# Low parts of four weight blocks and the transpose of the global group's keys, moved to GpSimd and VectorE

## The chip, the cores and the metric

The kernel runs on one core of one Trainium2 chip. A core has a matrix engine (TensorE, PE in the profile, with its weight loads as PEld), a vector engine (VectorE, DVE), an activation engine (ScalarE, ACT), a general engine (GpSimd, POOL) and a queue engine that here issues all DMAs (SyncE, SP). Each runs its own instructions in the order in which they were written, and they wait for each other through semaphores. The metric is the device time of one execution in microseconds (us); lower is better.

## The reference

A trunk of two layers over 256 tokens of width 1024, all in float32. Each layer:

- `h = rms_norm(x)`, then one projection to 2304 columns, which gives q, k, v of two groups of heads. Group A (MoBA, called the global group here) has 8 heads of 64 with their own keys; since the block size is 256 and the sequence 256, it is plain causal attention. Group B (SWA) has 8 query heads on 2 key/value heads, a window of 128 and one learned sink per head.
- rotary positions on q and k of both groups, softmax attention in each, an `rms_norm` of each group's output, and the output projection of the two side by side, normed and added to x.
- a SwiGLU block: gate and up projections to 2816 columns, `silu(gate) * up`, the down projection, normed and added to x.

## The kernel before

**Split products.** Every float32 product on PE is made of three: operands are split into a high part (rounded to the PE's fp32r type) and a low part (what is left), and high x high, high x low and low x high are accumulated. The weights come from memory in 46 blocks per layer (`BLOCKS`), each 128 x 2048: blocks 0 to 8 are the input projection, 9 to 12 the output projection, then gate/up and down. A block b is loaded by SP into one of three places of `raw` (`load_block`, L345 to L349), ACT copies it to the high part `w_h` (`hi`, L530 to L543), DVE subtracts to the low part `w_l` (`lo`, L790 to L794), and PE multiplies with both (`multiply`, L1147). `w_h` and `w_l` have four places each; `slot` gives the place, `before` the block that held it last. SP may load a block when the low part of the block three before it is made (`lo_ready`), ACT may copy it when PE has used the block four before.

**The order of work** is written out by hand for each engine. The projections come out in five pieces ci = 0 to 4 (SWA keys and values, SWA queries, MoBA keys, MoBA queries, MoBA values) for two tiles t of 128 tokens. Blocks 5 and 6 hold the MoBA queries (ci 3), 7 and 8 the MoBA values (ci 4). For each piece DVE runs `project` (L839: gain and bias, L855) and `rotate` (L860: the rotary products L877 and L878 and their sums L881 and L883, all four with both operands in SBUF), and counts `rotated`. PE then transposes the result with four 128 x 128 transposes (`qk`, L1225, through `transpose`, L1217), and ACT copies them from PSUM to `qT` or `kT` (`keep_qk`, L596 to L603). Bank 6 of PSUM holds all these in turn (`HOLDS`, L152).

**Attention** runs in three rounds per group (`ROUNDS`: tile 0, then two halves of tile 1). In each, PE makes `scores` (L1229), DVE the masked maxima (`maxima`, L902), ACT the exponentials into `probs` (`exps`, L614), PE transposes them (`probs_transposed`), ACT copies (`keep_probsT`, L630), and PE multiplies with the values (`values`, L1269). `normalise` (DVE, L920 to L922) divides by the sums: for SWA it first adds the sink's part to the row sums (L920, both operands in SBUF). ACT sums the squares (`sum_o`, L640), POOL makes the reciprocal root (`rms_o`, L485 to L491), DVE scales (`scale_o`, L932), PE transposes (`mix`).

**POOL** otherwise does only the roots of the norms in this stage. In the feed-forward stage it carries 32 x 128 pieces between partition groups (`exchange`, L493 to L503): there DVE transposes within 32 x 32 squares (`squares_f`, L983) and POOL's 16 copies per piece (L501) put the squares where a full transpose has them.

**The orders around the change.** On DVE in layer 0: `maxima(SWA, 0)`, `project(1, 1)`, the low parts of blocks 5 and 6, `normalise(SWA, 0)`, `maxima(SWA, 1)`, `project(2, 0)`, `project(2, 1)`, `project(3, 0)`, `maxima(SWA, 2)`, the low part of 7, `scale_o(SWA, 0)`, the low part of 8, `project(3, 1)`. In layer 1 `project(2, 0)` and the low part of 6 stand before `normalise(SWA, 0)`. On PE: `qk(1, 1)` follows `probs_transposed(SWA, 0, 1)`, then half of a block, `values(SWA, 0, ...)`, `scores(SWA, 1)`, and later `probs_transposed(SWA, 1, ...)`. On ACT the high part of block 7 follows `keep_qk(1, 1)`; the high part of 8 follows `exps(SWA, 1)` in layer 0 and the high part of 7 in layer 1.

Of the kernel before, what the change touches and what calls it, by code (L numbers as in the profile page):

```python
# [65 lines left out]

RAW = 3
# [78 lines left out]
for j in range(2):  # L146
    HOLDS[4 + j].append(("ht", 0, j, 1))
    for g in (SWA, MOBA):
        for r in range(3):
            HOLDS[4 + j] += [("scores", g, r, j), ("pt", g, r, j)]  # L150
    HOLDS[4 + j].append(("ht", 1, j, 1))
HOLDS[6] += [("ht", 0, 0, 0), ("qk", 0, 0), ("qk", 1, 0), ("qk", 0, 1), ("qk", 1, 1), ("qk", 2, 0), ("qk", 2, 1),  # L152
             ("qk", 3, 0), ("qk", 3, 1), ("mix", SWA, 0), ("mix", SWA, 1), ("mix", MOBA, 0), ("mix", MOBA, 1),
# [5 lines left out]
def trunk(nc, x_in, b_in, g_attn_pre, g_attn_post, g_moba, g_swa, sinks_in,  # L159
# [3 lines left out]
    with ExitStack() as ctx:  # L163
# [33 lines left out]
        squares = [work[:, 2 + t, :] for t in range(T)]  # L197
        crossed = [work[:, 4 + t, :] for t in range(T)]
# [44 lines left out]
        lo_ready = sem("lo_ready")  # L243
        block_used = sem("block_used")
# [20 lines left out]
        squares_ready = [sem(f"squares_ready{t}") for t in range(T)]  # L265
        crossed_in = [sem(f"crossed_in{t}") for t in range(T)]
# [61 lines left out]

        def tokens(t):
            return slice(t * P, (t + 1) * P)  # L330
# [8 lines left out]
        def _(sp):  # L339
# [5 lines left out]
            def load_block(L, b, wait=True):  # L345
                r = slot(b, RAW)
                if wait:
                    place_free(lo_ready, L * NB + before(b, RAW) + 1)
                sp.dma_start(raw[:, r, :], w_blocks[L, b]).then_inc(raw_in[r], 16)  # L349
# [35 lines left out]
            for L in range(depth):  # L385
                for b in range(RAW + 1, NB):
                    load_block(L, b)
                    if b == 6:
# [3 lines left out]

                        sp.dma_start(gain_b[:], broadcast(g_attn_post[L], D)).then_inc(gain_b_in, 16)
# [6 lines left out]
                    if b == 11:  # L400
                        projected(L, 2, 1)
                        load_bias(L, 4)
                    if b == 15:
# [26 lines left out]
        def _(pool):  # L430
# [73 lines left out]

            pool.wait_ge(const_ready, 8)
            rms_x(0, 0, 0)
            rms_x(0, 0, 1)
            for L in range(depth):
                rms_o(L, SWA, 0)
                rms_o(L, SWA, 1)  # L510
# [19 lines left out]
        def _(act):  # L530
# [65 lines left out]
            def keep_qk(L, ci, t):  # L596
# [3 lines left out]
                dst = (kT[SWA], qT[SWA], kT[MOBA], qT[MOBA])[ci]  # L600
# [71 lines left out]
            for L in range(depth):  # L672
# [27 lines left out]
                keep_qk(L, 2, 0)  # L700
                exps(L, SWA, 2)
                sink_exps(L, 1)
                keep_qk(L, 2, 1)
# [76 lines left out]
        def _(dve):  # L780
# [9 lines left out]
            def lo(L, b):  # L790

                dve.wait_ge(hi_ready, L * NB + b + 1)
# [67 lines left out]
            def rotate(L, ci, t, n):  # L860
# [6 lines left out]
                if (ci, t) in ((2, 1), (3, 0), (3, 1)):  # L867
                    past = {(2, 1): (1, 0), (3, 0): (1, 1), (3, 1): (2, 0)}[ci, t]
                    held = BANK_OF[("qk", *past)]
                    dve.wait_ge(full[held], HELD[held].done(L, ("qk", *past)))  # L870
# [5 lines left out]
                                     for m in (stage, rope_tmp))  # L876
# [7 lines left out]
                                        ALU.add).then_inc(rotated, 1)  # L884

# [121 lines left out]
            for L in range(depth):  # L1007
                if L == 0:
# [11 lines left out]
                    project(L, 2, 0)  # L1020
                else:
# [10 lines left out]
                    project(L, 2, 0)  # L1032
                    after(L, 2)
                    normalise(L, SWA, 0)
                    maxima(L, SWA, 1)
                project(L, 2, 1)
                if L:
                    after(L, 3)
                project(L, 3, 0)
                maxima(L, SWA, 2)  # L1040
# [427 lines left out]
```

## Time and profile before

| | us |
|---|---|
| median of 3 runs | 576.99 (576.70 to 577.41) |
| the profiled execution | 576.57 |
| its span, first to last instruction | 574.8 |
| PE busy in it | 566.5 (99%) |
| DVE busy | 374.3 (65%) |
| ACT busy | 293.9 (51%) |
| POOL busy | 232.3 (40%) |
| mean granted TensorE clock | 0.998 of full speed |

The span leaves out 1.8 us around the instructions. Busy is the union of an engine's instructions; matmuls are pipelined, and their ends are modelled, so that the start-to-start distance of two matmuls is what one costs.

### The profile page before, as it was taken

The page shows a single profiled execution, that of the slowest core. Times are in us where ns is not written, and L with a number is a line of the kernel's source. Part 1 is how long each engine was busy: PE and PEld are TensorE (multiplying, and loading weights), DVE is VectorE, ACT ScalarE, POOL GpSimd, SP SyncE. Part 2 cuts the span into 40 slices and gives each one's busy share as a digit, 9 for nine tenths or more (in the row PEclk, how much of TensorE's full clock was granted, in tenths as well). Part 3 has the DMA queues.
Part 4 walks back from the last instruction along what each step waited for, and adds up shares of the span by engine and source line. Part 5 has one row for each costly group of instructions (what it writes and reads, how often), then busy time and mean ns, then how long its engine had stood idle before and what let it go on. Part 6 is the DMA issues. An engine that isn't in the chain of part 4 may idle for free.

```text
span 574.8 us, 8319 instructions
## 1 busy us (share of the span) xinstructions
PE 566.5 (99%) x3107; PEld 467.0 (81%) x3107; DVE 374.3 (65%) x486; ACT 293.9 (51%) x420; POOL 232.3 (40%) x452
## 2 busy tenths in 40 slices
PE   8999999999999999999999999999999999999996
PEld 6777877888888889888888888778888888898884
DVE  6789875946745747265597987576846746645722
ACT  7575755664345354163546655674644354325420
POOL 1100001607797797800120000043297797799100
PEclk9999999999999999999999999999999999999999
DMA  8953642538555550478265443516565564352701
GB/s 304 389 205 123 237 148 109 222 114 315 202 211 196 175 215 29 193 285 303 91 238 200 158 164 131 201 47 247 218 258 192 174 217 178 119 220 81 286 1 74
DMA packets 18729, 107.32 MB, mean 187 GB/s; under 512 B 2816, under 2 KB 3072, under 8 KB 7168
## 3 DMA queue, kind: packets, MB, share of 16 engines
q1 hardware_dynamic: 18688, 106.78, 50.3%
q8 instruction: 25, 0.41, 0.3%
q14 instruction: 16, 0.13, 0.1%
HBM read 105.72 MB, written 1.05 MB: 186 GB/s over the span
## 4 chain that ended last, share of the span: by engine, by line
PE 88%; DVE 6%; DMA 3%; ACT 1%; issue 1%; DVEq 0%; POOLq 0%; SPq 0%; POOL 0%; ACTq 0%
PE bank L1177 81%; PE bank L1217 4%; DMA raw<-in_w_blocks 3%; PE bank L1269 2%; PE bank L1242 2%; DVE w_l L793 1%; DVE bank L902 1%; DVE work L855 1%; DVE work L877 1%; DVE work L878 1%; DVE work L943 0%; DVE w_l L807 0%; ACT w_h L543 0%; DVE work L883 0%; ACT work L592 0%
## 5 line engine op out<-in xcount | busy, mean ns | idle before, releaser
L793 DVE TENSOR_TENSOR w_l<-raw,w_h 128x2048 fp32r<-128x2048 f32 x90 | 206.1, 2298 | 115.5 <-ACT w_h L543 115.4
L1177 PE MATMUL bank<-w_h,actT_h 128*128 128x512 f32 (+1 forms) x600 | 230.3, 384 | 0.4 <-DVE work L855 0.3
L543 ACT ACTIVATE w_h<-raw 128x2048 fp32r<-128x2048 f32 x90 | 171.9, 1915 | 110.0 <-PE bank L1177 90.1
L1177 PE MATMUL bank<-w_h,actT_l 128*128 128x512 f32 (+1 forms) x600 | 225.6, 376 | 0.0
L1177 PE MATMUL bank<-w_l,actT_h 128*128 128x512 f32 (+1 forms) x600 | 225.2, 375 | 0.0
L501 POOL COPY work<-work 32x128 f32<-32x128 f32 (+1 forms) x384 | 191.6, 499 | 75.4 <-DVE work L983 59.6
L1177 PEld LDWEIGHTS bank<-w_h,actT_h 128*128 128x128 f32 x600 | 113.1, 188 | 23.6 <-issue 2.2
L1177 PEld LDWEIGHTS bank<-w_h,actT_l 128*128 128x128 f32 x600 | 112.9, 188 | 21.0
L1177 PEld LDWEIGHTS bank<-w_l,actT_h 128*128 128x128 f32 x600 | 113.1, 189 | 18.8
L488 POOL TENSOR_TENSOR norms<-norms,constants 128x1 f32<-128x1 f32 x8 | 1.5, 193 | 146.8 <-ACT bank L640 146.8
L1177 PE MATMUL bank<-w_h,fT_h 128*128 128x512 f32 x160 | 49.4, 390 | 0.0
L1177 PE MATMUL bank<-w_h,fT_l 128*128 128x512 f32 x160 | 49.3, 389 | 0.0
L1177 PE MATMUL bank<-w_l,fT_h 128*128 128x512 f32 x160 | 49.3, 389 | 0.0
L614 ACT ACTIVATE work<-bank,neg_max 128x128 f32<-128x128 f32 (+1 forms) x64 | 26.0, 426 | 23.3 <-DVE neg_max L902 23.2
L1177 PEld LDWEIGHTS bank<-w_h,fT_l 128*128 128x128 f32 x160 | 30.0, 188 | 6.3
L1177 PEld LDWEIGHTS bank<-w_l,fT_h 128*128 128x128 f32 x160 | 30.0, 188 | 6.2
L1177 PEld LDWEIGHTS bank<-w_h,fT_h 128*128 128x128 f32 x160 | 29.8, 188 | 6.0
L478 POOL TENSOR_TENSOR norms<-norms,constants 128x1 f32<-128x1 f32 x8 | 6.7, 836 | 69.2 <-ACT work L592 69.2
L578 ACT ACTIVATE fT_h<-work 128x512 fp32r<-128x512 f32 x20 | 12.5, 624 | 40.6 <-POOL work L501 40.6
L1217 PE MATMUL bank<-ident,work 128*128 128x128 f32 x228 | 32.5, 274 | 0.7 <-ACT work L614 0.5
L1217 PEld LDWEIGHTS bank<-ident,work 128*128 128x128 f32 x228 | 26.6, 140 | 7.8 <-ACT work L614 1.7
L990 DVE TENSOR_TENSOR fT_l<-work,fT_h 128x512 fp32r<-128x512 f32 x20 | 14.5, 725 | 19.1 <-ACT fT_h L578 19.1
(77 smaller groups left out, 403.1 us busy)
## 6 DMA issues: line engine op xcount, KB each, us to landing
raw<-in_w_blocks SPq DMA_DIRECT2D x90, 1024.0 KB, 4.8
bias<-in_b_in SPq DMA_DIRECT2D x8, 256.0 KB, 5.6
raw<-in_w_blocks SPq DMA_DIRECT2D x4, 256.0 KB, 5.2
raw<-in_w_blocks SPq DMA_DIRECT2D x2, 512.0 KB, 7.6
x<-in_x SPq DMA_DIRECT2D x2, 512.0 KB, 10.5
gain_b<-in_g_attn_post SPq DMA_DIRECT2D x2, 512.0 KB, 7.4
bias<-in_g_ffn_pre SPq DMA_DIRECT2D x2, 512.0 KB, 5.5
gain_b<-in_g_ffn_post SPq DMA_DIRECT2D x2, 512.0 KB, 5.8
```

The costliest lines, as they stand in the source:

```text
L478: link(L, nc.gpsimd.tensor_tensor(ss_y[:, t, 0:1], ss_y[:, t, 0:1], eps, ALU.add))
L501: ins = nc.gpsimd.tensor_copy(crossed[t][32 * j:32 * j + 32, i * n:(i + 1) * n], squares[t][32 * i:32 * i + 32, j * n:(j + 1) * n])
L543: nc.scalar.activation(w["h"][:, slot(b), :], raw[:, r, :], ACT.Copy).then_inc(hi_ready, 1)
L578: nc.scalar.activation(f_part("h", c, t), f_view(c, t), ACT.Copy).then_inc(f_hi_ready, 1)
L614: last = nc.scalar.activation(probs[:, j, n * keys:(n + 1) * keys], bank[4 + j][:, n * keys:(n + 1) * keys], ACT.Exp, bias=neg_max[:, g, t ...
L793: nc.vector.tensor_tensor(w["l"][:, slot(b), :], raw[:, slot(b, RAW), :], w["h"][:, slot(b), :].bitcast(F32), ALU.subtract).then_inc(lo_re ...
L855: nc.vector.scalar_tensor_tensor(dst[:, 0:n], bank[b][:, 0:n], rstd_x[:, t:t + 1], bias[:, ci % 2, 0:n], ALU.mult, ALU.add).then_inc(drain ...
L990: nc.vector.tensor_tensor(f_part("l", c, t), f_view(c, t), f_part("h", c, t).bitcast(F32), ALU.subtract).then_inc(f_lo_ready, 1)
L1177: ins = nc.tensor.matmul(bank[BANK_OF[name]][:, 0:n], left[s][:, at + k, tokens(t)], right[r][:, k, c * BANK:c * BANK + n], start=first an ...
L1217: ins = nc.tensor.transpose(out_[:, q * P:(q + 1) * P], src(q), ident[:])
L1242: ins = nc.tensor.matmul(bank[4 + j][:, n * keys:(n + 1) * keys], qT[g][side, i, tokens(t)], kT[g][side, i if g == MOBA else 0, 0:keys], s ...
L1269: ins = nc.tensor.matmul(bank[b][rows, h * HEAD:(h + 1) * HEAD], probsT[:, j, at + side * HEAD:at + (side + 1) * HEAD], v[g][:, kb, cols], ...
```

## The change

Four things. POOL computes the low parts of blocks 5 to 8 of each layer, as the first instructions of its layer, and signals them on a semaphore of its own; DVE's `lo` skips them; PE and SP wait for whichever engine makes the block's low part. The MoBA keys (ci 2) are no longer transposed by PE and copied by ACT: DVE transposes their 32 x 32 squares into `gain_b`, and POOL carries the squares to `kT` with 16 copies per tile, the two tiles between `rms_o(SWA, 0)` and `rms_o(SWA, 1)`. The load of `gain_b` (the gain after attention) moves on SP's queue from behind block 6 to behind block 11, where it waits for both tiles' keys; block 12 and all that follow on the queue stand behind it. On DVE `maxima(SWA, 2)` moves ahead of `project(3, 0)`.

```diff
+POOL_LOW = (5, 6, 7, 8)
...
+        k_squares = [gain_b[:, t * GROUP:(t + 1) * GROUP] for t in range(T)]
...
+        def low_done(L, b):
+            mine = [c for c in range(NB) if (c in POOL_LOW) == (b in POOL_LOW)]
+            return pool_lo_ready if b in POOL_LOW else lo_ready, L * len(mine) + mine.index(b) + 1
...
@@ SP: load_block, and the load of gain_b
-                    place_free(lo_ready, L * NB + before(b, RAW) + 1)
+                    last = before(b, RAW)
+                    place_free(*low_done(L + last // NB, last % NB))
...
                     if b == 6:
...
-                        sp.dma_start(gain_b[:], broadcast(g_attn_post[L], D)).then_inc(gain_b_in, 16)
...
                     if b == 11:
                         projected(L, 2, 1)
                         load_bias(L, 4)
+                        place_free(k_crossed, T * (L + 1))
+                        sp.dma_start(gain_b[:], broadcast(g_attn_post[L], D)).then_inc(gain_b_in, 16)
...
@@ POOL
+            def lo(L, b):
+                pool.wait_ge(hi_ready, L * NB + b + 1)
+                nc.gpsimd.tensor_tensor(w["l"][:, slot(b), :], raw[:, slot(b, RAW), :],
+                                        w["h"][:, slot(b), :].bitcast(F32), ALU.subtract).then_inc(pool_lo_ready, 1)
+
+            def cross_k(L, t):
+                pool.wait_ge(k_squares_ready, T * L + t + 1)
+                pool.wait_ge(rstd_o_ready, R_O.done(L, (SWA, 0)))
+                square = k_squares[t].rearrange("p (i c b) -> p i c b", i=4, b=32)
+                for a in range(4):
+                    for c in range(4):
+                        at = t * P + 32 * a
+                        ins = nc.gpsimd.tensor_copy(kT[MOBA][32 * c:32 * c + 32, :, at:at + 32],
+                                                    square[32 * a:32 * a + 32, :, c, :])
+                ins.then_inc(k_crossed, 1)
+                pool.wait_ge(k_crossed, T * L + t + 1)
...
             for L in range(depth):
+                lo(L, 5)
+                lo(L, 6)
+                lo(L, 7)
+                lo(L, 8)
                 rms_o(L, SWA, 0)
+                cross_k(L, 0)
+                cross_k(L, 1)
                 rms_o(L, SWA, 1)
...
@@ ACT
-                keep_qk(L, 2, 0)
...
-                keep_qk(L, 2, 1)
...
@@ DVE
             def lo(L, b):
+                if b in POOL_LOW:
+                    return
...
+            def square_k(L, t):
+                dve.wait_ge(rotated, turned(L, (2, t)))
+                nc.vector.transpose(k_squares[t], roped[2, t]).then_inc(k_squares_ready, 1)
...
                     project(L, 2, 0)
+                    square_k(L, 0)
...
                 project(L, 2, 1)
+                maxima(L, SWA, 2)
+                square_k(L, 1)
                 if L:
                     after(L, 3)
                 project(L, 3, 0)
-                maxima(L, SWA, 2)
...
@@ PE
-                        pe.wait_ge(lo_ready, L * NB + b + 1)
+                        pe.wait_ge(*low_done(L, b))
...
-                for name in (last_q, last_k):
-                    landed(L, name)
+                landed(L, last_q)
+                if g == SWA:
+                    landed(L, last_k)
+                else:
+                    pe.wait_ge(k_crossed, T * L + t + 1)
...
-                qk(L, 2, 0)
...
-                qk(L, 2, 1)
```

## Rows read from the trace of the kernel before

**Rows 1.** The page, part 4: the chain that ended last, shares by engine.
```profile
PE 88%; DVE 6%; DMA 3%; ACT 1%; issue 1%; DVEq 0%; POOLq 0%; SPq 0%; POOL 0%; ACTq 0%
```

**Rows 2.** Who PE waited for: total us, times, longest; the second largest of three.
```profile
PE bank L1217 <- ACT work L614: 0.5, 2, 0.3
```

**Rows 3.** Timeline of PE around one group of four transposes: start, length, engine, line.
```profile
28.86 0.40 PE L1177 MATMUL bank<-w_l,actT_h 128*128 128x512 f32 x1
29.10 0.39 PE L1177 MATMUL bank<-w_h,actT_l 128*128 128x512 f32 x1
...
30.00 0.39 PE L1177 MATMUL bank<-w_l,actT_h 128*128 128x512 f32 x1
```

**Rows 4.** Low parts and square transposes on DVE; copies on POOL (ns min/median/max).
```profile
L793 DVE TENSOR_TENSOR w_l<-raw,w_h 128x2048 fp32r<-128x2048 f32 x90 | 206.1, 2298 | 115.5 <-ACT w_h L543 115.4
...
L983 DVE STREAM_TRANSPOSE work<-work 128x512 f32<-128x512 f32 x20 | 14.0, 702 | 0.0
...
L501 POOL COPY work<-work x384: 226/288/2442, 132.5 to 532.4; 32x128 f32<-32x128 f32 x160, 32x64 f32<-32x64 f32 x32
```

**Rows 5.** Timeline, narrow windows of the feed-forward stage: POOL copies beside DVE's low parts.
```profile
134.16 0.28 POOL L501 COPY work<-work 32x128 f32<-32x128 f32 x1
...
134.23 2.36 DVE L793 TENSOR_TENSOR w_l<-raw,w_h 128x2048 fp32r<-128x2048 f32 x1 [1.14 <-ACT w_h L543]
...
134.48 2.26 POOL L501 COPY work<-work 32x128 f32<-32x128 f32 x1
...
529.92 2.32 DVE L793 TENSOR_TENSOR w_l<-raw,w_h 128x2048 fp32r<-128x2048 f32 x1
530.13 2.20 POOL L501 COPY work<-work 32x64 f32<-32x64 f32 x1
```

**Rows 6.** Timeline of layer 0, 30 to 47 us, by engine (ACT, DVE, PE).
```profile
30.46 3.71 ACT L543 ACTIVATE w_h<-raw 128x2048 fp32r<-128x2048 f32 x2
...
39.16 1.91 ACT L543 ACTIVATE w_h<-raw 128x2048 fp32r<-128x2048 f32 x1
44.21 0.48 ACT L614 ACTIVATE work<-bank,neg_max 128x256 f32<-128x256 f32 x1 [3.13 <-DVE neg_max L902]
...
35.78 0.69 DVE L877 TENSOR_TENSOR work<-work,sin 128x512 f32<-128x512 f32 x1
...
37.45 0.42 DVE L883 TENSOR_TENSOR work<-work 128x256 f32<-128x256 f32 x1
...
42.19 0.16 DVE L920 TENSOR_TENSOR row_sum<-row_sum,sink_exp 128x8 f32<-128x8 f32 x1
...
37.55 1.04 PE L1217 MATMUL bank<-ident,work 128*128 128x128 f32 x8
...
39.90 1.15 PE L1269 MATMUL bank<-v_swa,work 128*64 128x64 f32 x32
...
46.27 0.49 PE L1217 MATMUL bank<-ident,work 128*128 128x128 f32 x3
```

**Rows 7.** Timeline of layer 1, 307 to 328 us, by engine (ACT, DVE, PE).
```profile
307.68 1.92 ACT L543 ACTIVATE w_h<-raw 128x2048 fp32r<-128x2048 f32 x1 [0.41 <-PE bank L1177]
...
320.49 3.71 ACT L543 ACTIVATE w_h<-raw 128x2048 fp32r<-128x2048 f32 x2
...
315.26 0.69 DVE L877 TENSOR_TENSOR work<-work,sin 128x512 f32<-128x512 f32 x1
...
322.49 0.16 DVE L920 TENSOR_TENSOR row_sum<-row_sum,sink_exp 128x8 f32<-128x8 f32 x1
...
318.89 1.04 PE L1217 MATMUL bank<-ident,work 128*128 128x128 f32 x8
...
327.60 0.38 PE L1217 MATMUL bank<-ident,work 128*128 128x128 f32 x2
```

**Rows 8.** Start-up matmuls of PE (busy us, mean ns); the last stretch (its PEclk is 0.78).
```profile
L1211 PE MATMUL bank<-work 128*128 128x512 bf16 x10 | 4.4, 631 | 1.5 <-DVE work L993 1.5
...
569.20:574.80 5.60, 0.00 (x0) 0.00 (x0) 2.12 (x4) 0.65 (x2) 0.74 (x2) 0.78 0.25 95
```

More of the change, by code:

```diff
@@ L151 @@
     HOLDS[4 + j].append(("ht", 1, j, 1))
-HOLDS[6] += [("ht", 0, 0, 0), ("qk", 0, 0), ("qk", 1, 0), ("qk", 0, 1), ("qk", 1, 1), ("qk", 2, 0), ("qk", 2, 1),
-             ("qk", 3, 0), ("qk", 3, 1), ("mix", SWA, 0), ("mix", SWA, 1), ("mix", MOBA, 0), ("mix", MOBA, 1),
+HOLDS[6] += [("ht", 0, 0, 0), ("qk", 0, 0), ("qk", 1, 0), ("qk", 0, 1), ("qk", 1, 1), ("qk", 3, 0), ("qk", 3, 1), ("mix", SWA, 0), ("mix", SWA, 1), ("mix", MOBA, 0), ("mix", MOBA, 1),
              ("ht", 1, 0, 0)]
@@ L243, in trunk @@
         lo_ready = sem("lo_ready")
+        pool_lo_ready = sem("pool_lo_ready")
         block_used = sem("block_used")
@@ L265, in trunk @@
         squares_ready = [sem(f"squares_ready{t}") for t in range(T)]
+        k_squares_ready = sem("k_squares_ready")
+        k_crossed = sem("k_crossed")
         crossed_in = [sem(f"crossed_in{t}") for t in range(T)]
@@ L599, in keep_qk @@
                 act.wait_ge(full[b], HELD[b].done(L, ("qk", ci, t)))
-                dst = (kT[SWA], qT[SWA], kT[MOBA], qT[MOBA])[ci]
+                dst = {0: kT[SWA], 1: qT[SWA], 3: qT[MOBA]}[ci]
                 n = dst.shape[1]
@@ L868, in rotate @@
                     past = {(2, 1): (1, 0), (3, 0): (1, 1), (3, 1): (2, 0)}[ci, t]
-                    held = BANK_OF[("qk", *past)]
-                    dve.wait_ge(full[held], HELD[held].done(L, ("qk", *past)))
+                    if past == (2, 0):
+                        dve.wait_ge(k_squares_ready, T * L + 1)
+                    else:
+                        held = BANK_OF[("qk", *past)]
+                        dve.wait_ge(full[held], HELD[held].done(L, ("qk", *past)))
                 dve.wait_ge(drained[b], HELD[b].done(L, ("proj", ci, t)) + 1)
@@ L1032, in _ @@
                     project(L, 2, 0)
+                    square_k(L, 0)
                     after(L, 2)
@@ L1233, in scores @@
                 last_q, last_k = (("qk", 1, t), ("qk", 0, t)) if g == SWA else (("qk", 3, t), ("qk", 2, t))
[L1234 to L1235 removed]
+                landed(L, last_q)
+                if g == SWA:
+                    landed(L, last_k)
+                else:
+                    pe.wait_ge(k_crossed, T * L + t + 1)
                 for j in range(2):
```

## The prediction, made before the changed kernel had run

> **What bounds the kernel now.** I read the chain that ended last first: 88% of it is PE [rows 1], and the table of times has PE busy for 566.5 of 574.8 us. The list of waits comes next, and for this stage it holds one entry, 0.5 us for ACT's exponentials [rows 2]. So PE is fed without a pause, and only two things can move the time: instructions that leave PE, and waits that arrive at it. DVE's 65% is no bound, and what it is freed of is worth nothing by itself. But PE runs in a written order, and some of DVE's results reach it with almost nothing to spare, so after the chain I read the timelines at those places [rows 6, 7].
>
> **What leaves PE.** Four groups of four transposes (MoBA keys, two tiles, two layers). Two neighbouring matmuls start 0.23 to 0.24 us apart; with four transposes between, the second matmul after them starts 0.90 us after the one ahead of them [rows 3]. 0.90 less two such distances (0.46) is 0.44 us for a group, and four groups are 1.76 us, all on the path. ACT loses four copies that nobody on the path waits for: nothing.
>
> **What moves from DVE to POOL.** DVE loses eight low parts of 2.3 us (18.4 us) and gains four square transposes of 0.70 us [rows 4]. Neither is on the path. POOL gains eight two-operand instructions of 128 x 2048 and 64 copies. A copy of 128 elements takes 288 ns (median), one of 64 takes 226 ns (the least) [rows 4]: 0.97 ns an element and 0.16 us fixed. A subtraction of 2048 elements is at least 2.15 us (if both operands stream together) and 4.1 us if they come one after the other. The trace has no large two-operand instruction on POOL. I take 4.1, since every row there is a one-operand copy at one element in 0.97 ns, and keep 2.15 as the lower end. The Trainium skill (GPSIMD Engine Reference, section 3.1) says the two read streams share one port and gives 4497 ns for this size; by it each would be 0.4 us longer, and the sum about 1 us higher.
>
> By plain durations all of it is hidden. In layer 0 block 5's high part ends at 32.4 and 6's at 34.2 [rows 6]; POOL would end their low parts at 36.5 and 40.7, and PE takes block 5 at 42.1 and block 6 behind it. The 16 copies of a tile start 0.33 us apart (134.16 and 134.48 [rows 5]), 5.3 us a tile.
>
> **The port.** Rows 5 say more. A POOL copy that starts at 134.48, while DVE subtracts (134.23 to 136.59), takes 2.26 us in place of 0.29: it stands still until DVE has ended. The other direction is there too: the copy ahead started at 134.16, and DVE's subtraction, which started 0.07 us later, took 2.36 against 2.29 us; it was held until about 0.14 us into the copy, half its length, which is its reading. Both engines want one read path when DVE reads two operands from SBUF, and whoever has it keeps it. And they alternate: at 529.92 DVE goes from one subtraction into the next, and the copy that had waited gets in between. DVE instructions with one operand in PSUM (L855, the maxima, L922) aren't touched.
>
> With copies this costs DVE 0.1 us. With POOL subtractions of 4.1 us it costs up to 4 us for one DVE instruction, and the four of `rotate`, `scale_o`, and L920 of `normalise` are of that kind. The Trainium skill (SBUF — State Buffer, section "Who interferes with whom") states it as a lock that the first one holds for its whole instruction, which speaks against this change; the trace agrees for copies (2.26 us for 0.29) and shows nothing of POOL holding it long.
>
> **Layer 0, worked out.** The low part of 5 runs on POOL from 32.4 to 36.5. DVE reaches L877 of piece (1, 1) at 35.78 [rows 6] and waits to 36.4 (POOL's reading ends 0.15 before its end). The low part of 6 has been ready since 34.2, so POOL takes the path after L877 (37.0 to 41.1), and L878 waits to 41.0. POOL has nothing then (block 7's high part stands behind `keep_qk(1, 1)` on ACT), and the last three end at 42.5 instead of 37.87 (37.45 + 0.42). PE's `qk(1, 1)` is the second half of the eight transposes at 37.55, at 38.0 [rows 6]: 0.1 us of slack. So PE stands **4.5 us**. Behind it everything shifts by that. After it, `normalise` and the low part of 7 meet (below); if `normalise` is first, the exponentials are in time. The low part of 8 (51.8 to 55.9) holds up L877 of piece (2, 1) by 2.4 us and so `maxima(SWA, 2)`: another 0.2 us at the transposes of its probabilities, which are the tight ones already [rows 2].
>
> **Layer 1.** Block 5's high part ends at 309.6 [rows 7], its low part at 313.75, that of 6 at 317.9. DVE's L877 of (1, 1) stood at 315.26; it waits to 317.75, and the rest is unhindered: 2.5 us late, against transposes at 318.89 whose second half starts at 319.32 [rows 7] and rotated values that were there at 317.35. PE stands 0.55 us. Then block 7's high part ends at 323.0 (22.4 of the row at 320.49, and 0.6 later), and POOL takes the path to 327.1. DVE, with `project(2, 0)` and the square transpose ahead, reaches L920 at 323.5: it waits to 327.0. From L920 to the first exponentials of that round takes 2.0 us (42.19 to 44.21) and to the first two another 0.95 [rows 6]: 329.9. PE wants them at 327.60 + 0.55 [rows 7], so it stands **1.75 us**. The low part of 8 then ends at 331.3, 7 us ahead of its use.
>
> **TensorE's clock.** At the start ten matmuls take 631 ns each over 4.4 us, on the lower level (1.2 GHz), where the same work later goes twice as fast [rows 8]: 2.1 us lost. In the last 5.6 us, with PE idle, the granted clock is 0.78 in the mean [rows 8], so it fell within it. A stand of 4.5 us in layer 0 is of that kind; I count one fall, **2.1 us**, with zero as the other end. The 1.75 us of layer 1 is short of it.
>
> **The keys and the queue.** POOL's copies for tile 0 start at about 57 in the shifted layer 0, take 5.3 us and some 1.5 for DVE's instructions, and end at 63; `scores(MOBA, 0)` comes at 64.4 + 3.8. Nothing. `rms_o(SWA, 1)` stands behind tile 1's copies (72), before `sum_o` at 74. On SP, block 12 waits for them too, 4 to 6 us later than before, and its high part has over 5 us to spare; `gain_b` isn't wanted before the output projection ends. Nothing. Earlier frees of the raw places (low parts of 7 and 8 no longer behind DVE's order) are worth nothing where no DMA is waited for.
>
> **The sum**, against the profiled execution of 576.57 us: less 1.76, plus 4.5 and 0.2, plus 0.55 and 1.75, plus 2.1: 583.9. The median of the three runs is 0.4 above that execution: **584.2 us**. No fall of the clock takes 2.1 off: 582.1.
>
> **Rivals.** (1) *The path isn't held for a long POOL instruction* (it lets DVE in between, or DVE goes first). Then the gain stands alone: 576.99 - 1.76 = 575.2. For it: no row shows POOL holding the path over 0.15 us. Against it: the hold lasts as long as the copy's reading to within 0.05 us. This is the one on the other side; it decides if DVE's L877 in layer 0 ends within 0.7 us of its start, since beyond 0.1 us of slack each us of hold is a us of PE. Chance 0.22. (2) *POOL's subtraction is near 2.15 us*: the low parts of 5 and 6 end at 34.6 and 36.7, L877 waits 0.8 us, PE stands 0.7; L920 in layer 1 waits 1.5, within the slack. The gain is about eaten: 576 to 578. For it, a faster two-operand path than I assume. Chance 0.13, of it 0.08 within 0.2%, 0.05 above. (3) *The race in layer 0.* Block 7's high part ended at 41.07 (39.16 + 1.91) and the last product of `values` lands at about 41.1 [rows 6]; both follow PE's transposes, so they stay equal in the change. If POOL is first, L920 waits 3.7 us, the exponentials come 1.8 us late for PE (wanted at 46.27 [rows 6], shifted), everything behind moves, and the low part of 8 then delays `maxima(SWA, 2)` by another 2: 588.0. Chance 0.17. (4) The forecast, 582 to 586.5: 0.48.
>
> **The numbers.** Slower by over 0.2% (1.15 us, about what a measurement of this kernel can tell from no change): 0.48 + 0.17 + 0.05 = 0.70. Same: 0.08. Faster: 0.22. The two signs are apart, so the range has to reach from rival 1 to rival 3: 575.0 to 588.5, which leaves out about one in eight. The likeliest case's own range is 582 to 586.5.
>
> **What would show it.** Right: a POOL subtraction of about 4 us; L878 of piece (1, 1) in layer 0 at over 4 us in place of 0.68; PE waiting for L1217's operands from DVE, 4 to 5 us once; L920 in layer 1 at 3.5 us; a granted clock under 1 near 43 us. Wrong: `rotate` instructions near 0.7 us while POOL subtracts; PE waits below 3 us in all. If PE waits for the keys' copies, the step on their 5.3 us has failed; if it waits for low parts, the step on their dates.

## The result and the profile after

The changed kernel takes **592.1 us** (median of 6 runs, 591.13 to 592.81) against 577.42 us for the kernel before on the same chip (6 runs, 576.70 to 578.02): 1.0256 times as long, 95% interval 1.0242 to 1.0269. The prediction was 584.2 us, in a range up to 588.5. So the direction was right, and the loss of 14.7 us is twice the forecast 7.2. The profiled execution took 592.04 us, span 590.1, mean granted clock 0.989.

The page of the changed kernel, parts 1, 4 and 5 (busy us, share, instructions; then chain shares, which answer to [rows 1]; then groups). Line numbers have moved: `lo` is L518 on POOL and L828 on DVE; `project` L890; the products of `rotate` L915 and L916, its sums L919 and L921; the sink's argument in `maxima` L952; `normalise` L963; `exps` L649; `sum_o` L675; the transposes L1263.
```profile
PE 569.2 (96%) x3091; PEld 467.8 (79%) x3091; DVE 381.0 (65%) x482; ACT 292.1 (49%) x416; POOL 289.1 (49%) x524
...
PE 84%; DVE 9%; DMA 2%; issue 2%; ACT 1%; DVEq 0%; POOLq 0%; SPq 0%; POOL 0%; ACTq 0%
...
L518 POOL TENSOR_TENSOR w_l<-raw,w_h 128x2048 fp32r<-128x2048 f32 x8 | 36.5, 4579 | 38.0 <-ACT w_h L578 38.0
```
DVE's share of the chain has risen, though DVE has lost eight low parts. A subtraction on POOL is 4.58 us, about twice DVE's 2.30.

Whom PE waited for in the changed kernel (total us, times, longest), against [rows 2]:
```profile
PE bank L1263 <- DVE work L921: 6.7, 2, 5.4
PE bank L1263 <- ACT work L649: 4.4, 5, 2.3
PE bank L1257 <- DVE work L1036: 1.5, 1, 1.5
PE bank L1318 <- ACT bank L675: 1.3, 1, 1.3
```
The 1.5 us at L1257 is the start, as before. The rest is new or has grown: rotated queries that come late (L921), exponentials that come late (L649, 0.5 us before), and a sum of squares that frees a PSUM bank late (L675). No wait for the keys' copies is in the whole list: the 32 copies of layer 0 run from 63.84 to 78.80, and POOL is then idle for 1.85 us before the root of (SWA, 1).

Layer 0, timeline by engine (POOL, DVE, PE); these rows answer to [rows 6]:
```profile
32.61 9.09 POOL L518 TENSOR_TENSOR w_l<-raw,w_h 128x2048 fp32r<-128x2048 f32 x2 [7.50 <-ACT w_h L578]
47.32 4.57 POOL L518 TENSOR_TENSOR w_l<-raw,w_h 128x2048 fp32r<-128x2048 f32 x1 [5.62 <-ACT w_h L578]
...
35.09 2.16 DVE L952 TENSOR_TENSOR sink_exp<-sinks,neg_max 128x8 f32<-128x8 f32 x1
37.17 0.74 DVE L890 SCALAR_TENSOR_TENSOR work<-bank,norms,bias 128x512 f32<-128x512 f32 x1
37.95 4.30 DVE L915 TENSOR_TENSOR work<-work,sin 128x512 f32<-128x512 f32 x1
42.17 0.68 DVE L916 TENSOR_TENSOR work<-work,cos 128x512 f32<-128x512 f32 x1
...
43.23 0.41 DVE L921 TENSOR_TENSOR work<-work 128x256 f32<-128x256 f32 x1
...
49.04 2.87 DVE L963 TENSOR_TENSOR row_sum<-row_sum,sink_exp 128x8 f32<-128x8 f32 x1 [5.40 <-PE bank L1318]
...
43.70 1.12 PE L1263 MATMUL bank<-ident,work 128*128 128x128 f32 x4 [5.38 <-DVE work L921]
...
45.04 0.63 PE L1223 MATMUL bank<-w_l,actT_h 128*128 128x512 f32 x1
45.47 0.63 PE L1223 MATMUL bank<-w_h,actT_l 128*128 128x512 f32 x1
```
Read it from the top. Block 5's low part starts at 32.61. At 35.09 DVE comes to an instruction of 128 x 8 elements, which it ends in 0.17 us elsewhere, and stands 2.16 us, until that low part has been read. Then L890, which reads PSUM, runs freely. POOL has gone on to block 6, and L915 stands with it: it ends at 42.25, its own 0.69 us counted from 0.14 us before POOL's end at 41.70. PE gets its queries at 43.70 and has stood 5.38 us. Behind that, matmuls that were 0.23 us apart are 0.43 apart. And block 7's low part starts at 47.32, before DVE comes to L963: held again.

Layer 1, the same three engines; these rows answer to [rows 7]:
```profile
319.81 9.17 POOL L518 TENSOR_TENSOR w_l<-raw,w_h 128x2048 fp32r<-128x2048 f32 x2 [14.05 <-ACT w_h L578]
334.15 9.10 POOL L518 TENSOR_TENSOR w_l<-raw,w_h 128x2048 fp32r<-128x2048 f32 x2 [5.17 <-ACT w_h L578]
...
325.13 4.40 DVE L915 TENSOR_TENSOR work<-work,sin 128x512 f32<-128x512 f32 x1
...
334.60 4.17 DVE L963 TENSOR_TENSOR row_sum<-row_sum,sink_exp 128x8 f32<-128x8 f32 x1
...
330.98 0.66 PE L1263 MATMUL bank<-ident,work 128*128 128x128 f32 x4 [1.36 <-DVE work L921]
...
341.80 0.83 PE L1263 MATMUL bank<-ident,work 128*128 128x128 f32 x4 [2.33 <-ACT work L649]
...
342.86 0.63 PE L1223 MATMUL bank<-w_l,actT_h 128*128 128x512 f32 x1
343.29 0.63 PE L1223 MATMUL bank<-w_h,actT_l 128*128 128x512 f32 x1
```
And the granted clock, from the table by stretches of the changed kernel (stretch, length, busy us of PE, PEld, DVE, ACT, POOL, then PEclk, DMA share, GB/s). In the kernel before it was 1.00 over 36 to 56 and over 320 to 350.
```profile
36.00:43.70 7.70, 2.32 (x15) 1.79 (x14) 7.57 (x6) 2.59 (x11) 5.70 (x2) 0.87 0.48 161
43.70:47.30 3.60, 3.60 (x10) 2.56 (x10) 0.00 (x0) 2.40 (x2) 0.00 (x0) 0.50 0.81 330
47.30:49.00 1.70, 1.70 (x35) 1.63 (x34) 0.00 (x0) 0.00 (x0) 1.68 (x1) 0.64 0.00 0
...
340.00:346.00 6.00, 4.20 (x22) 3.38 (x23) 5.05 (x13) 3.15 (x12) 5.68 (x6) 0.72 0.57 232
```
0.50 is the lower level, 1.2 GHz. The clock fell in the long stand of layer 0 (a stand is a time in which PE waits), and a second time in layer 1, behind stands of 1.4 and 2.3 us.

**Where the 15.3 us of the span went** (590.1 less 574.8). Each row is how much the distance between one matmul and its counterpart of the kernel before grew at that place:

| place | us |
|---|---|
| L0, `qk(1, 1)` | +5.54 |
| L0, lower clock, 43.7 to 49 | +2.26 |
| L0, exponentials of (SWA, 1) | +0.69 |
| L0, `values(SWA, 1)` behind `sum_o` | +1.32 |
| L0, exponentials of (SWA, 2) | +1.07 |
| L1, `qk(1, 1)` | +1.52 |
| L1, exponentials of (SWA, 1) | +2.49 |
| L1, lower clock, 342 to 346 | +1.6 |
| four groups of transposes gone | -1.60 |
| the rest (start-up and drift) | +0.4 |

### The profile page after: what moved, and what is told of

It is laid out like the page before. It is cut to its first block, busy times and chain, and to the rows that moved or that the text cites. A ratio compares the mean times of both kernels' runs of the same rounds, so it can differ in the third digit from the quotient of the medians.

```text
span 590.1 us, 8355 instructions
## 1 busy us (share of the span) xinstructions
PE 569.2 (96%) x3091; PEld 467.8 (79%) x3091; DVE 381.0 (65%) x482; ACT 292.1 (49%) x416; POOL 289.1 (49%) x524
## 3 DMA queue, kind: packets, MB, share of 16 engines
HBM read 105.72 MB, written 1.05 MB: 181 GB/s over the span
## 4 chain that ended last, share of the span: by engine, by line
PE 84%; DVE 9%; DMA 2%; issue 2%; ACT 1%; DVEq 0%; POOLq 0%; SPq 0%; POOL 0%; ACTq 0%
PE bank L1223 77%; PE bank L1263 4%; DVE work L915 2%; DMA raw<-in_w_blocks 2%; PE bank L1318 2%; PE bank L1291 2%; DVE row_sum L963 1%; DVE bank L945 1%; DVE work L890 1%; DVE work L916 1%; DVE w_l L842 0%; DVE work L986 0%; DVE work L919 0%; DVE work L921 0%; ACT work L649 0%
## 5 line engine op out<-in xcount | busy, mean ns | idle before, releaser
L828 DVE TENSOR_TENSOR w_l<-raw,w_h 128x2048 fp32r<-128x2048 f32 x82 | 188.2, 2303 | 123.2 <-ACT w_h L578 123.2
L511 POOL COPY work<-work 32x128 f32<-32x128 f32 (+1 forms) x384 | 183.5, 478 | 75.4 <-DVE work L1026 59.6
L518 POOL TENSOR_TENSOR w_l<-raw,w_h 128x2048 fp32r<-128x2048 f32 x8 | 36.5, 4579 | 38.0 <-ACT w_h L578 38.0
L1263 PE MATMUL bank<-ident,work 128*128 128x128 f32 x212 | 31.9, 281 | 11.3 <-DVE work L921 6.7
L649 ACT ACTIVATE work<-bank,neg_max 128x128 f32<-128x128 f32 (+1 forms) x64 | 26.0, 426 | 32.2 <-DVE neg_max L945 32.2
L1263 PEld LDWEIGHTS bank<-ident,work 128*128 128x128 f32 x212 | 25.2, 143 | 19.6 <-DVE work L921 7.2
L529 POOL COPY kT<-gain_b 32x128 f32<-32x128 f32 x64 | 27.5, 430 | 3.6 <-POOL kT L529 0.8
```

The lines of the kernel that those rows point to most:

```text
L511: ins = nc.gpsimd.tensor_copy(crossed[t][32 * j:32 * j + 32, i * n:(i + 1) * n], squares[t][32 * i:32 * i + 32, j * n:(j + 1) * n])
L518: nc.gpsimd.tensor_tensor(w["l"][:, slot(b), :], raw[:, slot(b, RAW), :], w["h"][:, slot(b), :].bitcast(F32), ALU.subtract).then_inc(pool_ ...
L529: ins = nc.gpsimd.tensor_copy(kT[MOBA][32 * c:32 * c + 32, :, at:at + 32], square[32 * a:32 * a + 32, :, c, :])
L649: last = nc.scalar.activation(probs[:, j, n * keys:(n + 1) * keys], bank[4 + j][:, n * keys:(n + 1) * keys], ACT.Exp, bias=neg_max[:, g, t ...
L828: nc.vector.tensor_tensor(w["l"][:, slot(b), :], raw[:, slot(b, RAW), :], w["h"][:, slot(b), :].bitcast(F32), ALU.subtract).then_inc(lo_re ...
L1263: ins = nc.tensor.transpose(out_[:, q * P:(q + 1) * P], src(q), ident[:])
```

## The experiments

Differences are against the kernel before on the same chip (medians of 577.3, 577.24, 577.01 and 577.08 us beside the four groups of kernels, in this order: the two halves with lows_56_keys and lows_78_keys; low_write_only, low_one_read, low_in_8 and pe_filled; low6_waits, keys_spread and keys_tile_1; the three with block 9 later). Edits are to the changed kernel unless another base is named.

### The two halves of the change apart

**keys_only**: DVE keeps all low parts; the keys go by squares and POOL.
```diff
-POOL_LOW = (5, 6, 7, 8)
+POOL_LOW = ()
```


> POOL_LOW is empty: DVE makes all low parts again, the keys still go over the square transposes and POOL's copies. Theory (POOL's 4.6 us subtractions hold the read path that DVE's two-operand instructions need): no subtraction on POOL, no DVE instruction held for over 0.7 us, PE's waits of 5.4 and 2.5 us gone. The gain of the sixteen transposes (1.8 us) less what DVE's new order costs: the low part of block 7 ended at 57.9 against a use at 58.6, now moves 1.4 us later and the use 0.9 earlier, so about 1.6 us of waiting in layer 0: 576 to 578. Rival (the keys' copies and the new order on DVE cost the time): 585 or more.

**lows_only**: the kernel before, with the low parts of 5 to 8 on POOL as in the change, and nothing else.

> The kernel before with the four low parts on POOL and nothing else. Theory: the same holds as in the changed kernel, and the transposes of the keys back on PE (1.8 us): 591 to 596. Rival (the keys cost the time): 576 to 579.

keys_only took 581.42 us (5 runs; ratio 1.0073, 1.006 to 1.0086): slower by 4.1, a miss. lows_only took 595.23 (4 runs; 1.0316, 1.029 to 1.0342): slower by 17.9, inside what was expected. Together they give 14.7, not 22, for two reasons that the traces show. Where POOL makes the low part of block 7, what DVE does for the keys can't delay it. And lows_only pays 3.2 us at the exponentials of (SWA, 2) in layer 0, where the change pays 1.07: it has DVE's old order, and `maxima(SWA, 2)` stands behind both the held `rotate` and `project(3, 0)`. So the fourth part of the change, the maxima moved ahead, saves about 2 us (read from the two traces; no run moves it alone). In keys_only PE waits for
```profile
PE bank L1221 <- DVE w_l L826: 2.6, 2, 1.5
PE bank L1261 <- ACT work L647: 2.4, 3, 1.1
```
the low part of block 7 once per layer, and exponentials. The stretch from 35 to 69 us in layer 0, of the kernel before and of keys_only (columns as above), says why:
```profile
35.00:69.00 34.00, 33.50 (x267) 26.89 (x266) 33.03 (x72) 21.93 (x61) 1.06 (x2) 1.00 0.45 169
```
```profile
35.00:69.00 34.00, 31.79 (x254) 25.35 (x253) 33.27 (x65) 19.56 (x50) 18.32 (x32) 1.00 0.41 157
```
DVE is busy for 33.0 of these 34 us already before the change. Its 65% is a mean over the kernel; here it is 97% busy, nearly as full as PE, and two square transposes of 0.70 us now stand ahead of block 7's low part. PE takes that block 1.66 us later in layer 0.

### Which low parts, and which wait

**lows_56_keys** and **lows_78_keys**: only two of the four on POOL.
```diff
-POOL_LOW = (5, 6, 7, 8)
+POOL_LOW = (5, 6)      # lows_56_keys
+POOL_LOW = (7, 8)      # lows_78_keys
```


> Only blocks 5 and 6 on POOL, with the keys' new way. Theory: the waits at piece (1, 1) stay (5.5 us and the clock's 2.3 in layer 0, 1.5 in layer 1), those at normalise and at the second projection go, DVE pays 4.6 us more for blocks 7 and 8 in its full stretch: 583 to 588. If every subtraction cost PE the same, it would be half of the change's loss, 584.5, too; the trace then tells them apart by where PE waits.

> Only blocks 7 and 8 on POOL, with the keys' new way. Theory: no wait at qk(1, 1) in either layer (rotate of (1, 1) at its old lengths), but the row-sum addition of normalise(SWA, 0) held by the low part of 7 in both layers, 2 to 4 us of PE each time: 579 to 585, and no stretch at half clock near 44 us, since PE never stands 5 us.

One run each: 590.51 and 585.46 us, 2.5 and 0.5 us above what was expected. With 5 and 6 on POOL PE stands for DVE's L919 6.7 us in two waits, 5.4 the longest, the very numbers of the full change; and, as in keys_only, 1.6 and 1.4 us at the low part of block 7 and 1.05 and 1.25 at the exponentials of (MoBA, 1), more than was expected of a full DVE. With 7 and 8 that wait is gone, and PE is 3.5 us later at the exponentials of (SWA, 1) in layer 0 and 3.2 in layer 1. There the two engines alternate: POOL's low part of 7 starts behind a DVE subtraction, and DVE's L961 behind it.
```profile
38.82 4.49 DVE L826 TENSOR_TENSOR w_l<-raw,w_h 128x2048 fp32r<-128x2048 f32 x2
43.23 4.57 DVE L961 TENSOR_TENSOR row_sum<-row_sum,sink_exp 128x8 f32<-128x8 f32 x1
...
42.18 5.58 POOL L518 TENSOR_TENSOR w_l<-raw,w_h 128x2048 fp32r<-128x2048 f32 x1 [16.22 <-ACT w_h L576]
```
POOL's instruction is a microsecond longer than its 4.58, which is what was left of DVE's. Then DVE's 128 x 8 takes 4.57.

### What of a POOL instruction holds DVE

Three kernels keep the change's places and semaphores and give POOL another instruction.

**low_write_only**: POOL only writes. The low parts of blocks 5 to 8 are left out of the computation.
```diff
-                nc.gpsimd.tensor_tensor(w["l"][:, slot(b), :], raw[:, slot(b, RAW), :],
-                                        w["h"][:, slot(b), :].bitcast(F32), ALU.subtract).then_inc(pool_lo_ready, 1)
+                nc.gpsimd.memset(w["l"][:, slot(b), :].bitcast(F32), 0.0).then_inc(pool_lo_ready, 1)
```


> In the changed kernel POOL writes zeros to the low parts of blocks 5 to 8 in place of subtracting, so these low parts are left out of the products. POOL is still busy for some 2 us at each, at the same places, and signals the same; only its reading of SBUF is gone. Theory (the read path): no DVE instruction held, PE waits as in the kernel before, 575 to 577. Rival (a POOL instruction of any kind on SBUF, or its semaphores, hold DVE up): L877's counterpart in piece (1, 1) held for about the length of a write, and 580 or more.

**low_one_read**: POOL copies, with one operand read. These blocks' low parts are replaced by the blocks themselves.
In place of the subtraction:
```diff
+                nc.gpsimd.tensor_copy(w["l"][:, slot(b), :], raw[:, slot(b, RAW), :]).then_inc(pool_lo_ready, 1)
```


> In the changed kernel POOL copies the raw block to the low part of blocks 5 to 8 in place of subtracting the high part, so the products of these blocks are left wrong. One operand read, not two. By the copies' 0.97 ns an element it takes 2.15 us and holds DVE's two-operand instructions for up to 2.1 us. Theory: in layer 0 the low parts of 5 and 6 end at 34.7 and 36.9 and the rotate of (1, 1) is held 1 us at most: PE loses 1 to 3 us in all: 576 to 580. Rival (any POOL work of the size costs the same): 590.

**low_in_8**: the same subtraction in eight pieces of 256 columns.
Again in place of the subtraction:
```diff
+                for q in range(8):
+                    cols = slice(q * BLOCK // 8, (q + 1) * BLOCK // 8)
+                    ins = nc.gpsimd.tensor_tensor(w["l"][:, slot(b), cols], raw[:, slot(b, RAW), cols],
+                                                  w["h"][:, slot(b), cols].bitcast(F32), ALU.subtract)
+                ins.then_inc(pool_lo_ready, 1)
```


> In the changed kernel each low part on POOL is eight subtractions of 256 columns. POOL's work grows by its fixed part, the longest hold falls from 4.5 to about 0.6 us. Theory (a hold lasts one instruction and the two engines alternate): every DVE two-operand instruction waits at most 0.6 us; rotate of (1, 1) is late by some 2 us in place of 5.8, PE doesn't stand long enough for the clock to fall: 578 to 583. Rival (the path is lost for as long as POOL has work queued, or the loss goes with POOL's total reading): 590 or more.

| kernel | POOL, one instruction | in all | time, us | against before |
|---|---|---|---|---|
| low_write_only | 1.81 us, no read | 14.5 | 575.88 | -1.36 |
| low_one_read | 1.90 us, one read | 15.1 | 578.21 | +0.97 |
| low_in_8 | 0.84 us, two reads | 51.2 | 583.70 | +6.5 |
| the change | 4.58 us, two reads | 36.5 | 592.10 | +14.7 |

(One run each but for the change; the kernel before spreads over 1.2 us beside them. The first two are inside what was expected, low_in_8 is 0.7 us above it.) The group of POOL's L518 in low_write_only, and from its timeline a DVE instruction of two SBUF operands that starts while POOL is at work (33.24 to 36.85):
```profile
L518 POOL MEMSET w_l<- 128x2048 f32 x8 | 14.5, 1808 | 39.8 <-ACT w_h L577 39.8
```
```profile
35.74 0.17 DVE L951 TENSOR_TENSOR sink_exp<-sinks,neg_max 128x8 f32<-128x8 f32 x1
```
The same two of low_one_read (POOL at work from 33.79 to 37.54):
```profile
L518 POOL CAST w_l<-raw 128x2048 fp32r<-128x2048 f32 x8 | 15.1, 1900 | 42.2 <-ACT w_h L577 42.2
```
```profile
36.28 1.27 DVE L951 TENSOR_TENSOR sink_exp<-sinks,neg_max 128x8 f32<-128x8 f32 x1
```
The same DVE instruction at the same place is free beside a POOL instruction that only writes, and held to the end of one that reads. It isn't the only one: in low_write_only eight DVE instructions with two SBUF operands overlap a write of POOL, and none is over 0.03 us longer than in the kernel before; in low_one_read five are held, by 0.1 to 1.7 us (the longest is the 128 x 8 of `normalise`, 1.89 us). The Trainium skill (SBUF — State Buffer, "Who interferes with whom") says this: a DVE instruction with two SBUF inputs contends with a GpSimd instruction that reads SBUF, and not with one that only writes. This pair of rows agrees. And low_in_8 has more POOL work than the change and costs less than half, since DVE nearly always gets a turn after the piece under way (its L918 takes 1.21 us in place of 0.69, not 4.3). It did not once: at 49.74 L918 takes 2.12 us, over two more pieces, so that turns are the usual case and no rule. The price goes with the length of one POOL instruction and not with their sum. One thing expected of low_in_8 failed: behind a stand of 2.0 us, where PE waits for `qk(1, 1)`, the granted clock is 0.65 over 41 to 44 us.

low_write_only is the only kernel here that ends below the kernel before, by 1.36 us where the transposes are worth 1.6 to 1.76. One run within a spread of 1.2 us would say little, but its trace agrees: from 28 us to the end PE gains 1.74 us on the kernel before. It can't be used: its low parts are missing.

### Can a wait give DVE its turn?

**low6_waits**: POOL begins block 6 only when DVE has rotated (1, 1).
```diff
                 lo(L, 5)
+                pool.wait_ge(rotated, turned(L, (1, 1)))
                 lo(L, 6)
```


> The changed kernel, but POOL starts the low part of block 6 only when the rotate of piece (1, 1) has ended. Theory (holds, one per turn): in layer 0 the sink argument still waits for the low part of 5 (2.2 us), but no subtraction stands behind it, so rotate (1, 1) is 2.2 us late and not 5.8, PE stands 2 us and not 5.4; in layer 1 the 4.4 us hold of that rotate goes. The later holds at normalise and the second projection stay. 3.4 + 1.5 us less than the changed kernel, 586 to 589; the clock's fall in layer 0 may go too, but pe_filled has shown that this gives nothing there. Rival (POOL's amount of work sets the loss, wherever it stands): 591 or more.

594.19 us (4 runs; 1.0298, 1.0282 to 1.0314), a miss: slower than the change. PE's wait for `qk(1, 1)` fell from 5.4 to 1.8 us in layer 0 and is gone in layer 1, as meant. But the POOL instructions had only moved. Its timeline in layer 1 (DVE, then POOL), and the first of PE's waits:
```profile
326.91 4.21 DVE L916 TENSOR_TENSOR work<-work,sin 128x512 f32<-128x512 f32 x1
331.04 0.68 DVE L917 TENSOR_TENSOR work<-work,cos 128x512 f32<-128x512 f32 x1
331.75 4.70 DVE L920 TENSOR_TENSOR work<-work 128x256 f32<-128x256 f32 x1
336.38 4.71 DVE L922 TENSOR_TENSOR work<-work 128x256 f32<-128x256 f32 x1
...
325.96 4.60 POOL L518 TENSOR_TENSOR w_l<-raw,w_h 128x2048 fp32r<-128x2048 f32 x1 [2.89 <-DVE work L922]
331.29 9.52 POOL L518 TENSOR_TENSOR w_l<-raw,w_h 128x2048 fp32r<-128x2048 f32 x2 [0.72 <-ACT w_h L579]
```
```profile
PE bank L1264 <- ACT work L650: 12.1, 3, 8.4
```
Three subtractions one behind the other hold three DVE instructions of one `rotate` by 3.5, 4.3 and 4.3 us, one each. Only L917 is free, in the 0.7 us in which POOL waits for ACT. `normalise` is behind them, and PE stands 8.4 us for its exponentials. In layer 0 the exponentials of (SWA, 2) come 3.6 us late in place of 1.07, and behind both of these stands the clock falls again, which costs about another 2.9 and 1.6 us. The time is the one that the rival foretold (POOL's amount of work sets the loss), but low_in_8, with more POOL work and 8.2 us less loss, speaks against it as the cause.

### TensorE's clock

**pe_filled**: in layer 0 18 matmuls without use keep PE at work ahead of `qk(1, 1)`, in layer 1 8 of them ahead of the transposes of (SWA, 1).
```diff
+            def fill(L, n, following):
+                pe.wait_ge(drained[6], HELD[6].before(L, following) + 1)
+                for _ in range(n):
+                    nc.tensor.matmul(bank[6][:], actT["h"][:, 0, tokens(0)], actT["h"][:, 0:2, :],
+                                     start=True, stop=True)
...
+                if L == 0:
+                    fill(L, 18, ("qk", 1, 1))
                 qk(L, 1, 1)
...
+                if L:
+                    fill(L, 8, ("qk", 3, 0))
                 probs_transposed(L, SWA, 1, 0)
```


> The changed kernel with matmuls whose result is thrown away in PE's two long stands: 18 ahead of qk(1, 1) in layer 0 (4.2 us of 5.4) and 8 ahead of the transposed probabilities of the second round in layer 1 (1.8 us of 2.5). They lengthen no wait; they keep PE busy. Theory: the clock stays at its upper level, and the time at the lower one (some 2.3 us in layer 0, 1.5 in layer 1) is given back, and in layer 0 normalise meets the low part of 7 less late: 587 to 589.5. Rival (the slow matmuls behind the stands have another cause, or the fillers take as long as they give): 592 or more.

590.52 us (4 runs, 588.38 to 591.19; 1.0217, 1.0194 to 1.024): 13.3 us above the kernel before where the change is 14.7 above it, between the two expectations. The same stretches as above:
```profile
36.00:44.00 8.00, 7.20 (x35) 5.41 (x33) 7.90 (x7) 3.60 (x17) 6.80 (x2) 1.00 0.55 189
44.00:48.00 4.00, 3.20 (x44) 2.59 (x46) 0.76 (x3) 2.40 (x2) 0.03 (x1) 1.00 0.78 313
...
340.00:350.00 10.00, 9.41 (x75) 7.27 (x74) 8.36 (x25) 5.28 (x19) 9.26 (x16) 1.00 0.65 237
```
The clock stays at its upper level. In layer 0 that brings little, 0.4 us: the growth at `qk(1, 1)` is 5.63 us with the fillers, and that at the exponentials of (SWA, 1) becomes 2.44 in place of 2.26 of lower clock and 0.69 of wait, because L963 is held there (4.59 us) whatever PE does. In layer 1 the 1.6 us of lower clock come back. (In the profiled execution the start takes 1.0 us more than in that of the change, so that the two differ by 0.85 us and not by 2.) So of two falls one cost its price, and the other lay beside a wait. The falls don't come in every execution either: two of the change's six had a mean clock of 0.993 and 0.995 in place of 0.989, and took 591.13 us each.

### The keys by themselves

Three kernels without POOL's low parts look for the gain in the transposes.

**keys_spread**: keys_only with `maxima(SWA, 2)` back behind `project(3, 0)`, and tile 1's square transpose behind the low parts of 7 and 8.
```diff
                 project(L, 2, 1)
-                maxima(L, SWA, 2)
-                square_k(L, 1)
...
                 project(L, 3, 0)
+                maxima(L, SWA, 2)
...
                 after(L, 4)
+                square_k(L, 1)
```


> keys_only with DVE's old order (the maxima of the third SWA round behind piece (3, 0)) and the second square transpose behind the low part of block 8. Theory (keys_only lost 4.1 us because DVE, full from 35 to 69 us, was given 1.4 us more ahead of the low part of block 7, and its order delays it further): the low part of block 7 ends at about 58.6 against a use at 57.7, 0.9 us of waiting in layer 0 in place of 1.7 and less in layer 1: 577 to 579.5. Rival (the copies on POOL ahead of rms_o(SWA, 1) delay the second MoBA round's chain by about 1 us a layer): the waits of 1.0 and 1.3 us at its transposed probabilities stay, so not below 578.5.

**keys_tile_1**: the same, and only tile 1 goes by POOL; tile 0's keys are transposed by PE as before.

> Only tile 1's keys take the new way; tile 0's go over PE as before; DVE's old order, all low parts on DVE. Half of the transposes' gain (0.9 us) against 0.7 us of DVE work a layer behind the low part of block 8, and 16 copies a layer on POOL that can start at 61.5. Theory: the second MoBA round's chain, which already ended 0.4 us late for PE, moves by up to 0.7: 576.5 to 578. Rival (one tile fits without loss): 575.8 to 576.6, below the kernel before by the 0.9.

578.54 us (9 runs; 1.0032, 1.0022 to 1.0042) and 577.96 (11 runs; 1.0014, 1.0005 to 1.0023), both as expected. So 2.6 of keys_only's 4.1 us were the place of the second square transpose and of `maxima(SWA, 2)` on DVE; keys_spread puts back both, and which of them weighs more is not shown. What stays in keys_tile_1 is 0.40 us at the exponentials of (SWA, 2) and 1.05 at those of (MoBA, 1), at 80 us in layer 0. POOL's root of (SWA, 1) still follows ACT's sum at once, so the copies don't delay it; DVE itself reaches `normalise(SWA, 1)` later, since it has no idle time before.

That gave a last theory: take block 9's low part out of DVE's way.

**before_low9_later**, **tile_1_low9_later**, **spread_low9_later**: the kernel before, keys_tile_1 and keys_spread, each with
```diff
-                after(L, 5)
                 maxima(L, MOBA, 0)
                 normalise(L, SWA, 1)
                 project(L, 4, 0)
+                after(L, 5)
                 scale_o(L, SWA, 1)
```


> The kernel before, with DVE's low part of block 9 moved from ahead of the first MoBA maxima to behind the values' projection, where DVE stood idle for 1.85 us ahead of scale_o(SWA, 1). Theory (the second MoBA round's probabilities are late because DVE comes late to the first round's maxima and to the rest of that chain): PE's wait of some 0.4 us there shrinks, but the low part now delays scale_o by what of its 2.3 us the idle time doesn't hold: 576.3 to 577.5. Rival (DVE has room there): 575.8 to 576.3.

> keys_tile_1 with the same move. Theory: of the 1.0 us that PE waits there in each layer half or more goes, and the half gain of the transposes (0.9 us) shows: 576 to 577. Rival (the move only shifts the lateness to scale_o): 577.5 to 578.5.

> keys_spread with the same move. Theory: the wait at the second MoBA round shrinks as above, that of the third SWA round (1.3 us in layer 0, from the 0.7 us of the first square transpose in DVE's full stretch) stays: 577 to 578. Rival: 578.5 or more.

579.27 us (1.0038, 1.0024 to 1.0051), 578.68 (1.0032, 1.0019 to 1.0045) and 579.49 (1.0046, 1.0033 to 1.0058), 5 runs each: the theory fell. All three are slower, also without any keys on POOL. The timeline of before_low9_later (POOL, DVE) shows what replaced the wait:
```profile
71.33 1.26 POOL L488 TENSOR_TENSOR norms<-norms,constants 128x1 f32<-128x1 f32 x1 [20.57 <-ACT bank L640]
...
70.25 2.28 DVE L793 TENSOR_TENSOR w_l<-raw,w_h 128x2048 fp32r<-128x2048 f32 x1
```
POOL's root, an instruction of 128 x 1 that takes 0.19 us in the kernel before, stands 1.07 us until DVE's low part is done. It is the same exclusion the other way round. DVE, done with the low part, is idle for 0.71 us until the root is there, and `scale_o` and all of MoBA's second round wait for it: PE's matmul at 80 us comes 0.92 us later than its neighbours do, and 1.06 in layer 1. No version that computes the whole result was found below the kernel before.

## Why the direction was right and the size wrong

The direction and the mechanism (POOL holds DVE's two-operand instructions, and PE waits for them) were right; the sum was 8 us short. Two steps of it failed. The race in layer 0 was taken for even and left out of the sum, and cost 2.9 us more than the 0.2 that stood there. The second stand of layer 1 was taken as too short for the clock, put at nothing, and cost 1.6. The other 3 us are mostly terms of the right kind and too small, from POOL's subtraction (4.1 taken, 4.58 measured) and an instruction left out of DVE's order. One by one:

- **What bounds the kernel**: PE, fed with almost nothing to spare. Right: PE's new waits all come from DVE instructions that were held. The half sentence that DVE's 65% is no bound was wrong for 35 to 69 us, where it is 97% busy; keys_only showed it.
- **The transposes** (1.76): 0.44 and 0.36 a layer, 1.60. Right; low_write_only gives the whole effect, 1.36.
- **POOL's subtraction** (4.1 taken, 2.15 the lower end): 4.58. The Trainium skill's 4497 ns (GPSIMD Engine Reference, section 3.1), set aside for an estimate from this case's copies, was nearer. Two such subtractions stand ahead of each `qk(1, 1)`, so half a microsecond each counts twice.
- **The port** (whoever has it keeps it; they take turns): right, but for one turn missed in low_in_8. Both rows and the three kernels with another POOL instruction show it. Rival 1 (not held, 0.22) and rival 2 (near 2.15, 0.13) are out.
- **Layer 0, `qk(1, 1)`** (4.5): 5.5. I passed over an instruction: the sink's argument (L952), 128 x 8, two SBUF operands. I let L877 take the first turn between blocks 5 and 6, so that only L878 stood behind block 6. In fact that small one took it, and both products stood behind block 6, 0.6 us more. POOL's two durations would add 1.0, less the 0.5 that block 6 began earlier because the turn in between was so short.
- **Layer 1, `qk(1, 1)`** (0.55): 1.5. **Exponentials of (SWA, 1)** (1.75): 2.5. The places, the order and the instruction (L920, now L963) were right; POOL's duration makes all of the first difference (two subtractions, 0.5 us longer each) and most of the second (one).
- **The clock** (one fall, 2.1): it fell as predicted and cost 2.26 us at its place, but pe_filled shows that only 0.4 us of it counted in the end. "The 1.75 us of layer 1 is short of it" failed: the stand was 2.3 us behind one of 1.4, the clock fell, and pe_filled got that 1.6 back. The prediction went by the length of the stand alone, and the other runs show that this doesn't decide: in low_in_8 the clock fell behind one of 2.0 us, in lows_78_keys it stayed at 1.00 in layer 1 behind one of 3.0. What does decide stays open.
- **The race in layer 0** (rival 3, 0.17): it came, and not by chance. I had it even because both sides, I wrote, "follow PE's transposes, so they stay equal in the change". They don't, and the same prediction had the clock's fall that parts them: `values` runs on PE, which had the lower clock by then, and ended 7.9 us later than before (49.0 against 41.1), while ACT's high part of 7 ended 6.17 later (47.24 against 41.07). POOL was first by 1.7 us. The cost is 0.69, 1.32 and 1.07 us, 3.1 in all for the rival's 3.8. In pe_filled, at the upper clock, POOL starts 0.01 us ahead of DVE and DVE is still held: without the clock it is the even race that I took it for.
- **The keys and the queue** ("Nothing"): nothing in the change, where DVE has lost the low parts, but 4.1 us alone. The step counted the copies' end against their use and left out what the square transposes push back on a full DVE.

So the sum by terms: 1.0 more in layer 0, 1.0 and 0.7 more in layer 1, 2.9 of race (3.1 less the 0.2 that stood in the sum), 1.6 of a second fall, 0.2 more for the first, and 0.2 less gain from the transposes: 7.6. With the 0.4 of start-up and drift that is the distance of the profiled execution, 592.04, from the sum of 583.9, to within 0.2. The forecast and rival 3 were treated as alternatives around one duration, and the range ended at the rival's own best value, without the bounds of its other terms on top.

## What to carry to other kernels

Where GpSimd reads SBUF, every VectorE instruction with two SBUF operands, even one of 8 columns, can stand for one whole GpSimd instruction: list them all in the stretch, in order, before you give GpSimd long ones, and count a hold for each. Cutting the GpSimd instruction into pieces cut the price here, though it raised its total work; the wait that moved it only moved the hold. And read the busy share of an engine in the stretch that changes, not over the kernel: 0.7 us added to an engine that is 97% busy there is not free.

## What the runs showed of the hardware that I had not expected

- A hold doesn't scale with the work of the one held: 128 x 8 on DVE (0.17 us) took 2.16, 2.87, 4.17 and 4.59 us, and 128 x 1 on POOL (0.19 us) took 1.26.
- In eight pieces the same subtraction takes 6.4 us (51.2 us over eight blocks) in place of 4.58, with the turns that DVE takes included, and the loss is 8.2 us smaller (6.5 for 14.7).
- Matmuls at the lower clock started 0.43 us apart against 0.23, from the first one behind a stand of 5.4 us, and again behind one of 2.3 us, which came some 10 us after one of 1.4. The same shows in low_in_8 behind a stand of 2.0 us and not in layer 1 of lows_78_keys behind one of 3.0.
